# Matmul operands begin 96 bytes, instead of 64, in front of the weights' place modulo 256

## The chip, the core and the metric

The kernel runs on one core of one Trainium2 chip. The metric is the device time of one execution in microseconds. Before the change three runs took 1768.28, 1770.12 and 1774.59 us; the median is 1770.12.

## The reference, cut to what matters

Two models are computed one after the other for 256 tokens of 1024 numbers each, all in float32:

```
h = x
h = h + mamba2_mixer(rmsnorm(h))          # chunked state-space mixer: in, scan, out
h = h + conv_glu_ffn(rmsnorm(h))          # (silu(conv(h @ w_gate)) * (h @ w_up)) @ w_down, width 2816
h = h + fox_attention(rmsnorm(h))         # 16 heads with forget gates
h = h + conv_glu_ffn(rmsnorm(h))
h = rmsnorm(h)
h = [meta; h]                             # 16 meta tokens in front
h = h + [attention(latents); conv_group] @ w_out
h = h + peer_ffn(rmsnorm(h))              # 8 heads x 16 of 16384 experts: gelu(u . x) * gate, times v
out = rmsnorm(h)[16:272]
```

Nearly all of it is products of x with large weights. The experts are computed densely: every u is multiplied with every token (the U pass), the result is multiplied with gates that are zero but for the chosen experts, and then with every v (the V pass).

## The kernel before

**Three matmuls for one.** TensorE's one-pass float type (F32R) keeps fewer bits than float32. So each number is split into a high part of that type and a low part, the rest, and the helper `three` (L361 to L364) issues high by high, high by low and low by high. Profile lines L362, L363 and L364 are these three. A matmul here has a loaded operand of 128 x 128 and a moving operand that streams past it; in the profile's names `ps<-xc,hi` the moving one stands first. Each matmul has a weight load (PEld) of its own, which runs under the matmul before it.

**Weights.** They come from HBM in units of 128 x 2048 numbers (1 MB), in order, into a ring of three buffers `raw`. ScalarE writes the high part into `hi` (L584, L1549), GpSimd (POOL) the low part into `lo` (L759), and TensorE reads both. In the expert passes the units are halves of 1024 columns and two of the ring's buffers are used; ScalarE's part is L1767, the low part is POOL's in the U pass (L798) and VectorE's in the V pass (L2472). SyncE issues the loads when the slot's raw data have been split. The engines' orders are written out by hand and tied together with semaphores; a few loops have many rounds.

**Partners.** `pe_a` (L366) loads weights and streams x (`xc`, `xcl`: 8 chunks of 128 x 256). `pe_b` (L380) loads x and streams 256 weight columns. `pe_w` (L394) loads weights and streams the output halves `oh`, `ol` of a mixer, or the feed-forward products `hdh`, `hdl`. For the second model x has 272 columns (`xh`, `xl`, L165 and L167), rows of 1088 bytes; its query units stream weights of 256 or 160 columns, its convolution units stream 272 columns of x. `u_half` (L1329) is the U pass: 8 triples for each half unit; in its middle part each half unit is followed by gate products four small float32 matmuls (L1326). `v_pair` (L1377) is the V pass: it loads `wgh`, `wgl` (the gated activations, 128 of 256 tokens at a time) and streams 512 columns of `hi`, `lo`.

**Places.** All buffers of SBUF are placed by hand. `sb` puts a buffer at the running place and advances it by the buffer's bytes per partition, rounded up to 32; `to(n)` (L148) advances it to the next byte that is n modulo 256. `raw`, `hi` and `lo` begin at 128 modulo 256, `h` and `acc` too. `xh` and `xl` begin at 64 modulo 256 (`xc` and `xcl` lie in the same memory), and so do `xn`, `oh`, `ol`, four `tmp`, `ones` and the buffers of each phase, `hdh` and `hdl` among them (`xdh`, `xdl` for the routing weights as well). All steps from one chunk to the next are multiples of 256 bytes, but for the 1088 of `xh` and `xl`. The second pair of `wgh`, `wgl` lies in x's memory, 64 bytes on, at 128 modulo 256, as the first pair.

Of the kernel before, what the change touches and what calls it, by code (L numbers as in the profile page):

```python
# [16 lines left out]
F32R = mybir.dt.float32r  # L17
# [7 lines left out]
P = 128  # L25
D = 1024
KC = D // P
SEQ = 256
# [102 lines left out]
def build(nc, A, out):  # L131
# [3 lines left out]
    def sb(name, shape, dt=F32, at=None):  # L135
        size = int(np.prod(shape[1:])) * (2 if dt == BF16 else 4)
        size = (size + 31) // 32 * 32
        off = place["at"] if at is None else at
        t = nc.alloc_sbuf_tensor_at(name, shape, dt, offset=off)
        if at is None:  # L140
            place["at"] += size
        return t
# [5 lines left out]
    def to(offset):  # L148
        place["at"] += (offset - place["at"]) % 256
# [10 lines left out]
    for s in range(2):  # L160
        lo.append(sb(f"lo{s}", [P, UNIT], F32R))
    rs = sb("rs", [P, 3, 32])
    to(64)
    xh_at = place["at"]
    xh = sb("xh", [P, KC, T2], F32R)  # L165
    xl_at = place["at"]
# [8 lines left out]
    lo.append(sb("lo2", [P, UNIT], F32R))  # L175
    h = sb("h", [P, KC, SEQ])
    acc = sb("acc", [P, 2, SEQ])
    to(64)
    xn_at = place["at"]
    xn = sb("xn", [P, NT, D])  # L180
    oh = sb("oh", [P, 2, 2, SEQ], F32R)
# [7 lines left out]
    rrow = sb("rrow", [P, T2])  # L189
    rc = sb("rc", [P, 8])  # L190
    rows = sb("rows", [P, NROWS])
    to(64)
    phase = place["at"]

    def start_phase():
# [104 lines left out]
    hot_at = place["at"]  # L300
# [4 lines left out]
    assert place["at"] <= nc.sbuf_usable_end, (place["at"], nc.sbuf_usable_end)  # L305

    act_in = [sb(f"act_in{i}", [P, 2, SEQ], at=hot_at + 2048 * i) for i in range(2)]
    wgh = [sb(f"wgh{i}", [P, 2, SEQ], F32R, at=(hot_at + 4096, xh_at + 64)[i]) for i in range(2)]
    wgl = [sb(f"wgl{i}", [P, 2, SEQ], F32R, at=(hot_at + 6144, xh_at + 64 + 2048)[i]) for i in range(2)]

    hf = sb("hf", [P, NT, D], at=gates_at)
    gfin = sb("gfin", [P, D], at=gates_at + 8192)
# [2285 lines left out]
```

## Time and profile before

| | |
|---|---|
| three runs | 1768.28, 1770.12, 1774.59 us |
| median | 1770.12 us |
| profiled execution: its span | 1774.7 us |
| granted TensorE clock, mean | 0.978 |
| PE, PEld busy | 1710.5 us (96%), 1606.4 us (91%) |
| DVE, ACT, POOL busy | 1044.9, 826.9, 900.8 us |
| DMA | 310.79 MB, 175 GB/s in the mean |

The profiled execution's own time is its span, 1774.7 us, from the first to the last instruction; it stands beside 1774.59, the slowest of the three runs. PE is busy nearly throughout, but matmuls overlap, so that busy time says little of its pace: a matmul of 256 columns is shown as some 280 ns long and the next begins after less than half of that. The distance between starts is what to read, in a timeline or from the count in a stretch.

The stretches are, in us from the start: the state-space mixer to 245, the first feed-forward part to 441, fox attention to 611, the second feed-forward part to 802, the second model's mixer to 958, routing among other work and the U pass from 995 to 1413, the V pass to the end.

### The profile page before, as it was taken

How to read it: one execution, taken by the hardware profiler on the slowest of the kernel's cores; microseconds unless marked ns; L12 is line 12 of the kernel's file. 1: busy time of each engine (PE TensorE's matmuls, PEld its weight loads, DVE VectorE, ACT ScalarE, POOL GpSimd, SP SyncE). 2: the span in 40 equal slices, each digit the busy share in tenths (PEclk: the TensorE clock that was granted, in tenths of full speed). 3: DMA queues.
4: the chain of work that ended last, by engine and by line, in shares of the span. 5: the costliest groups of instructions: out<-in, count | busy, mean ns of one | idle time of the engine just before them, and what ended most of it. 6: DMA issues, size and time to landing. Idle time of an engine off the chain costs nothing. (4 is left out here: it accounts for less than half of the span.)

```text
span 1774.7 us, 34933 instructions
## 1 busy us (share of the span) xinstructions
PE 1710.5 (96%) x12583; PEld 1606.4 (91%) x12583; DVE 1044.9 (59%) x2198; ACT 826.9 (47%) x1147; POOL 900.8 (51%) x275
## 2 busy tenths in 40 slices
PE   8899799999999999999998999999999999999997
PEld 8889799999997999999678999999999978888886
DVE  7857654345344554344885891745555377777776
ACT  4578343334547433345435544644444443333332
POOL 4676468887682378876205588776666500000000
PEclk9999999999998999999988999999999999999999
DMA  5443335555452245554202466665555687777774
GB/s 212 143 144 118 113 126 190 190 188 192 143 190 72 72 167 190 188 183 160 93 1 84 164 234 236 210 205 177 178 177 177 216 266 240 240 241 243 239 242 160
DMA packets 77453, 310.79 MB, mean 175 GB/s; under 512 B 8768, under 2 KB 10304, under 8 KB 60736
## 3 DMA queue, kind: packets, MB, share of 16 engines
q1 hardware_dynamic: 75024, 306.14, 51.3%
q10 hardware_dynamic: 2352, 3.59, 0.6%
q8 instruction: 52, 0.85, 0.2%
q14 instruction: 25, 0.20, 0.0%
HBM read 290.82 MB, written 18.87 MB: 175 GB/s over the span
## 5 line engine op out<-in xcount | busy, mean ns | idle before, releaser
L759 POOL TENSOR_TENSOR lo<-raw,hi 128x2048 fp32r<-128x2048 f32 x127 | 584.3, 4610 | 378.1 <-ACT hi L584 306.0
L362 PE MATMUL ps<-xc,hi 128*128 128x256 f32 x1912 | 544.3, 285 | 5.7 <-DVE ps L2052 3.3
L363 PE MATMUL ps<-xcl,hi 128*128 128x256 f32 x1912 | 536.3, 280 | 0.0
L364 PE MATMUL ps<-xc,lo 128*128 128x256 f32 x1912 | 536.1, 280 | 0.0
L362 PEld LDWEIGHTS ps<-xc,hi 128*128 128x128 f32 x1912 | 362.6, 190 | 8.6 <-issue 6.9
L798 POOL TENSOR_TENSOR lo<-raw,hi 128x1024 fp32r<-128x1024 f32 x128 | 304.7, 2404 | 128.8 <-ACT hi L1767 128.7
L363 PEld LDWEIGHTS ps<-xcl,hi 128*128 128x128 f32 x1912 | 364.3, 191 | 0.1
L1767 ACT ACTIVATE hi<-raw 128x1024 fp32r<-128x1024 f32 x256 | 264.9, 1058 | 211.3 <-PE ps L364 199.0
L364 PEld LDWEIGHTS ps<-xc,lo 128*128 128x128 f32 x1912 | 360.6, 189 | 0.0
L2472 DVE TENSOR_TENSOR lo<-raw,hi 128x1024 fp32r<-128x1024 f32 x128 | 156.4, 1222 | 81.1 <-ACT hi L1767 81.0
L362 PE MATMUL ps<-hi,wgh 128*128 128x512 f32 x512 | 199.4, 389 | 1.8 <-DVE wgl L2483 1.8
L363 PE MATMUL ps<-lo,wgh 128*128 128x512 f32 x512 | 199.2, 389 | 0.0
L364 PE MATMUL ps<-hi,wgl 128*128 128x512 f32 x512 | 199.2, 389 | 0.0
L584 ACT ACTIVATE hi<-raw 128x2048 fp32r<-128x2048 f32 x65 | 124.5, 1915 | 68.1 <-PE ps L364 66.8
L1805 ACT ACTIVATE act_out<-ps 128x512 f32<-128x512 f32 x64 | 38.3, 598 | 200.9 <-PE ps L364 200.7
L1549 ACT ACTIVATE hi<-raw 128x2048 fp32r<-128x2048 f32 x60 | 114.4, 1907 | 13.2 <-PE ps L364 13.2
L2044 DVE TENSOR_TENSOR ps<-ps,rrow 128x512 f32<-128x512 f32 x44 | 30.8, 699 | 145.8 <-PE ps L364 145.7
L362 PEld LDWEIGHTS ps<-hi,wgh 128*128 128x128 f32 x512 | 96.1, 188 | 22.5 <-issue 1.6
L2453 DVE TENSOR_TENSOR oj<-iota,ps 128x512 f32<-128x512 f32 x64 | 44.0, 688 | 121.9 <-PE ps L1326 120.9
L1544 ACT ACTIVATE fcv<-fcv 128x256 f32<-128x256 f32 x44 | 18.4, 419 | 207.1 <-DVE fcv L2050 207.1
L364 PEld LDWEIGHTS ps<-hi,wgl 128*128 128x128 f32 x512 | 96.1, 188 | 20.0
L363 PEld LDWEIGHTS ps<-lo,wgh 128*128 128x128 f32 x512 | 96.1, 188 | 19.7
(497 smaller groups left out, 3426.6 us busy)
## 6 DMA issues: line engine op xcount, KB each, us to landing
raw<-in_w_u SPq DMA_DIRECT2D x128, 512.0 KB, 4.3
raw<-in_w_v SPq DMA_DIRECT2D x128, 512.0 KB, 4.2
raw<-in_w_up SPq DMA_DIRECT2D x44, 1024.0 KB, 4.8
raw<-in_w_down SPq DMA_DIRECT2D x22, 1024.0 KB, 4.7
raw<-in_w_fox SPq DMA_DIRECT2D x16, 1024.0 KB, 5.0
act_save<-act_out SPq DMA_DIRECT2D x64, 256.0 KB, 2.1
act_in<-act_save SPq DMA_DIRECT2D x64, 256.0 KB, 3.2
raw<-in_w_xbc SPq DMA_DIRECT2D x12, 1024.0 KB, 5.0
```

Of the source, the lines that this page charges most:

```text
L362: pe.matmul(o, ah, bh, start=start, stop=False)
L363: pe.matmul(o, ah, bl, start=False, stop=False)
L364: return pe.matmul(o, al, bh, start=False, stop=stop)
L584: nc.scalar.activation(hi[slot][:], raw[slot][:], ACT.Copy).then_inc(hi_done, 1)
L759: return g.tensor_tensor(lo[slot][:], raw[slot][:], hi[slot][:].bitcast(F32), ALU.subtract)
L798: g.tensor_tensor(lo[q // 2][:, part], raw[q // 2][:, part], hi[q // 2][:, part].bitcast(F32), ALU.subtract).then_inc(u_lo_done, 1)
L1549: s.activation(hi[slot][:], raw[slot][:], ACT.Copy).then_inc(hi_done, 1)
L1767: nc.scalar.activation(hi[s][:, q], raw[s][:, q], ACT.Copy).then_inc(e_hi_done, 1)
L1805: nc.scalar.activation(act_out[s][:].rearrange("p a b -> p (a b)"), ps[:, s, :], ACT.Gelu).then_inc(a_gelu, 1)
L2044: v.tensor_tensor(both, both, bc(rrow[:, META:], 1, [P, 2, SEQ]), ALU.mult).then_inc(f_chain, 1)
L2453: return v.tensor_tensor(place[b][:], iota[:].unsqueeze(1).broadcast_to([P, GT, P]), number, ALU.is_equal)
L2472: v.tensor_tensor(lo[s][:, q], raw[s][:, q], hi[s][:, q].bitcast(F32), ALU.subtract).then_inc(v_lo_done, 1)
```

## The change

The three `to(64)` become `to(32)`, and the second pair of `wgh`, `wgl` is put 96 instead of 64 bytes behind the beginning of x's memory. Nothing else is touched; no instruction is added or taken away.

```diff
@@ -160,7 +160,7 @@
     rs = sb("rs", [P, 3, 32])
-    to(64)
+    to(32)
     xh_at = place["at"]
@@ -175,7 +175,7 @@
     acc = sb("acc", [P, 2, SEQ])
-    to(64)
+    to(32)
     xn_at = place["at"]
@@ -189,7 +189,7 @@
     rows = sb("rows", [P, NROWS])
-    to(64)
+    to(32)
     phase = place["at"]
@@ -305,8 +305,8 @@
-    wgh = [sb(f"wgh{i}", [P, 2, SEQ], F32R, at=(hot_at + 4096, xh_at + 64)[i]) for i in range(2)]
-    wgl = [sb(f"wgl{i}", [P, 2, SEQ], F32R, at=(hot_at + 6144, xh_at + 64 + 2048)[i]) for i in range(2)]
+    wgh = [sb(f"wgh{i}", [P, 2, SEQ], F32R, at=(hot_at + 4096, xh_at + 96)[i]) for i in range(2)]
+    wgl = [sb(f"wgl{i}", [P, 2, SEQ], F32R, at=(hot_at + 6144, xh_at + 96 + 2048)[i]) for i in range(2)]
```

## Rows read from the trace of the kernel before

**Rows 1.** The page: span; chain that ended last, by line.

```profile
span 1774.7 us, 34933 instructions
...
PE ps L362 13%; PE ps L363 13%; PE ps L364 13%; PE ps L1326 3%; DVE eq L2441 1%; DVE eq L2443 1%; DVE sel L2444 1%; DMA act_in<-act_save 0%; POOL lo L798 0%; POOL lo L759 0%; ACT hi L584 0%; DVE h L2319 0%; ACT hi L1767 0%; DVE hf L2505 0%; DVE xdl L478 0%
```

**Rows 2.** Stretches: length, busy us (instructions) of PE, PEld, DVE, ACT, POOL; PEclk, DMA.

```profile
271.40:435.30 163.90, 163.90 (x1394) 163.90 (x1393) 69.51 (x140) 64.07 (x54) 134.23 (x30) 1.00 0.53 187
638.30:802.30 164.00, 164.00 (x1395) 164.00 (x1395) 69.60 (x140) 64.17 (x55) 134.37 (x30) 1.00 0.53 186
468.20:485.60 17.40, 17.40 (x151) 17.40 (x149) 8.52 (x37) 10.15 (x13) 14.30 (x4) 1.00 0.48 166
485.70:523.90 38.20, 38.20 (x338) 38.20 (x338) 20.72 (x86) 18.84 (x21) 31.59 (x8) 1.00 0.54 188
1001.30:1114.30 113.00, 113.00 (x959) 113.00 (x960) 69.28 (x307) 51.57 (x62) 96.42 (x41) 1.00 0.68 229
1159.40:1387.30 227.90, 227.90 (x1986) 227.90 (x1986) 116.75 (x186) 107.86 (x156) 149.29 (x64) 1.00 0.53 179
1391.00:1412.90 21.90, 21.90 (x196) 21.90 (x195) 3.44 (x5) 10.60 (x14) 14.29 (x6) 1.00 0.76 257
```

**Rows 3.** Groups by line and shape: names, shapes, count, busy us, mean ns, idle.

```profile
L362 PE MATMUL ps<-xc,hi 128*128 128x256 f32 x1912 | 544.3, 285 | 5.7 <-DVE ps L2052 3.3 <-issue 0.8 <-POOL lo L798 0.5
...
L362 PE MATMUL ps<-hi,wgh 128*128 128x512 f32 x512 | 199.4, 389 | 1.8 <-DVE wgl L2483 1.8
...
L362 PE MATMUL ps<-hi,xc 128*128 128x256 f32 x384 | 109.4, 285 | 0.3 <-DVE xcl L478 0.2
...
L362 PE MATMUL ps<-hdh,hi 128*128 128x256 f32 x352 | 98.9, 281 | 0.0
```

**Rows 4.** Timeline of PE between gate products: start us, us, instruction.

```profile
1159.79 0.28 PE L362 MATMUL ps<-xc,hi 128*128 128x256 f32 x1
...
1161.91 0.28 PE L362 MATMUL ps<-xc,hi 128*128 128x256 f32 x1
...
1163.52 0.28 PE L362 MATMUL ps<-xc,hi 128*128 128x256 f32 x1
...
1165.56 0.28 PE L362 MATMUL ps<-xc,hi 128*128 128x256 f32 x1
```

**Rows 5.** Timeline of PE at half clock.

```profile
812.39 0.41 PE L362 MATMUL ps<-hi,xh 128*128 128x256 f32 x1
...
813.03 0.41 PE L362 MATMUL ps<-hi,xh 128*128 128x256 f32 x1
```

**Rows 6.** Timeline of PE in the V pass.

```profile
1449.93 0.39 PE L362 MATMUL ps<-hi,wgh 128*128 128x512 f32 x1
...
1451.97 0.39 PE L362 MATMUL ps<-hi,wgh 128*128 128x512 f32 x1
```

**Rows 7.** The page, DMA issues: count, KB each, us to landing.

```profile
act_save<-act_out SPq DMA_DIRECT2D x64, 256.0 KB, 2.1
```

**Rows 8.** Timeline of PE, 272 columns, first of triples k=4 onward.

```profile
825.86 0.29 PE L362 MATMUL ps<-xh,hi 128*128 128x272 f32 x1
...
826.23 0.29 PE L362 MATMUL ps<-xh,hi 128*128 128x272 f32 x1
...
826.62 0.29 PE L362 MATMUL ps<-xh,hi 128*128 128x272 f32 x1
...
826.99 0.29 PE L362 MATMUL ps<-xh,hi 128*128 128x272 f32 x1
...
827.37 0.29 PE L362 MATMUL ps<-xh,hi 128*128 128x272 f32 x1
```

**Rows 9.** Timeline of PE, 160 columns.

```profile
818.92 0.28 PE L362 MATMUL ps<-hi,xh 128*128 128x160 f32 x1
...
819.92 0.27 PE L362 MATMUL ps<-hi,xh 128*128 128x160 f32 x1
```

**Rows 10.** Timeline of PE, eight convolution taps, full fp32.

```profile
870.11 1.89 PE L1186 MATMUL ps<-hc,diag 128*128 128x256 f32 x8
```

## Prediction

> **What bounds the kernel now.** I read the page's head and its chain of waits first [rows 1]. The span is 1774.7 us and the chain that ended last runs mostly through L362, L363 and L364, 13% each: these are the three matmuls of the helper that multiplies a number split into a high and a low part. So the pace of those matmuls is what counts. The table by stretches [rows 2] shows where: in both feed-forward parts, in the two fox query stretches, in the U pass of the experts and in its end, PE is busy for all of the stretch, and POOL, ACT and DVE for 85% of it at the most. The grouped instructions [rows 3] give the kinds: x (xc, xcl) streams as moving operand past loaded weights 1912 times for each of the three lines, the weights stream past loaded x 384 times, the feed-forward products hdh and hdl 352 times, all with 256 columns, and the V pass streams 512 columns 512 times. (The output halves oh and ol go the way of hdh.)
>
> The mean ns of those groups is no pace, because matmuls overlap. The pace is the distance between starts. In the U pass between the gate products, six triples take 2.12 us in one half unit, 117.8 ns each, and 2.04 us in the next, 113.3 ns each [rows 4]. Both read x from the same place, and weights from places that lie a multiple of 4096 bytes apart. The stretch table agrees (the window and 0.28 us of the matmul already under way, by the count): 117.8, 117.8, 117.1 and 118.1 ns in the first, second, third and fifth row, 113.8 and 113.2 ns in the fourth and the last [rows 2]. So there are two paces at the same offset of 64 bytes, a slow one and a fast one, and most of the time is spent in the slow one.
>
> What would be no excess at all? At half clock, 1.2 GHz, three starts take 0.64 us, 213 ns each [rows 5], which is 256 columns at 1.2 GHz and nothing more. At 2.4 GHz, the granted clock in nearly all the rest, 256 columns are 106.7 ns, so 6.7 or 11.1 ns are lost per matmul and only at full speed. That looks like the moving stream and the weight load, both reading SBUF at once, getting into each other's way. The V pass has both of its streams at 128 modulo 256 and takes 2.04 us for nine [rows 6], 226.7 ns against 213.3: 13.3 ns lost.
>
> **The change, part by part.** No instruction is added, removed or reordered, no wait and no DMA either. It only moves places. x, everything from xn to rows, and every phase's buffers begin 32 bytes lower; raw, hi, lo, h and acc stay, because the allocator rounds to 128 again behind x. With the sizes in the listing nothing else shifts: each of the three stops falls 32 bytes earlier and nothing wraps to the next 256.
>
> The weights for the V pass stay too: wgh1 and wgl1 lie at xh's place plus 64, now plus 96, which is 128 in both. V is 1536 matmuls [rows 3] at 226.7 ns, 348 us, and I cost it at nothing. act_out slides 32 bytes, and its 64 stores of 256 KB take 2.1 us each [rows 7], in a pass that needs 5.5 us or more for a unit, so a store that took twice as long would be hidden. DVE and ACT instructions on moved buffers read and write from another place; in the PE-bound stretches DVE is busy at most 61% of the time and ACT 58% [rows 2], so they could grow by half before they set the pace.
>
> What is left is the pace of some 8,000 matmuls of 256 columns. No row has its streams at 96 bytes apart, so I bound it by rows at other distances. The 272-column matmuls of the last block are of use: a row of x is 1088 bytes, so its place advances by 64 bytes with each k. Their triples take 0.37 us at minus 64, 0.39 at 0, 0.37 at plus 64 and 0.38 at 128 (k from 4 to 7) [rows 8]; without loss each would take 0.34. So place does matter, it repeats after 128 bytes as far as this shows, 64 (modulo 128) is the better and 0 the worse, by about 5 ns a matmul. A distance of 96 is 32 modulo 128: just between the two that are known.
>
> The lower end: with 160 columns the stream would take 67 ns, yet nine starts take 1.00 us, 111.1 ns each [rows 9]. There the weight load sets the pace, and no 256-column matmul can go below it by much. All at 111.1 ns: the four slow stretches, 163.9 + 164.0 + 17.4 + 113.0 = 458.3 us, lose 6.7 parts in 117.8, 26 us; the two fast ones, 38.2 + 21.9 us, lose 1.2; the gate stretch has about 31 pairs of half units (227.9 us, 3.73 from 1159.79 to 1163.52 for one with its gate products), of 24 matmuls each, 31 x 24 x (6.7 + 2.2) ns = 6.6 us; the rest some 4. That is 38 us less. The upper end is the worst triple, 0.39 us or 130 ns for 272 columns, 16.7 ns lost, so 123.3 ns for 256: 21 + 5 + 31 x 24 x (5.5 + 10.0) ns = 12 + 3, 41 us more.
>
> I take the value in between that the rows show to be possible in these very loops: every matmul at 113.3 ns. The four slow stretches give 458.3 x 4.5 / 117.8 = 17.5 us. The slow half units of the gate stretch give 31 x 24 x 4.5 ns = 3.3 us. Elsewhere some 2,000 matmuls of the groups are left; if all were slow and all on the path they would give 9 us, but these are the parts in which the matmuls stand in short runs between waits, and some run at 113.3 ns already, so I take 2. Sum: 23 us. POOL, 134.2 us in a stretch that would shrink from 163.9 to 157.7 us, remains below it. Why should 96 be on the good side? Suppose that a load begins some 3 ns behind the matmul it lies under, less than the timeline resolves: the moving stream, 4 bytes a column at 2.4 GHz, has then run on by some 28 bytes (an estimate). With that lag, 64 behind becomes some 36 behind and 0 becomes 28 ahead, nearly equally near to a meeting, which fits that the two differ so little in rows 8. 96 behind would be 64 to 70 behind, the farthest that two streams can be on a ring of 128 bytes. This is an argument, not a row.
>
> The profiled execution's span, 1774.7 us, is the slowest of the three times shown (1774.59); the median is 1770.1. 1774.7 - 23 gives 1751.7 for a like execution; on the median it is 1747.
>
> A rule of the Trainium skill speaks against all of this: SBUF — State Buffer, section Who interferes with whom, gives TensorE two independent read ports, one for the moving operand and one for weight loads, and says PE and ACT "never wait on anyone". By it the places cannot matter and the time stays at 1770 us. The trace disagrees, 0.37 against 0.39 us with nothing changed but k [rows 8].
>
> **The rivals.**
>
> No effect: the pace is set by how each run of matmuls happens to begin, not by the distance. For it speaks that both paces occur at one distance in neighbouring half units [rows 4]; against it rows 8. The time would be 1770, within 5 us.
>
> Slower: 96 is nearer to a meeting of the streams than 64. The mechanism: at 32 modulo 128 each load overlaps half of a piece that the moving stream is reading, and the fast pace is no longer reached. For it: linear interpolation in rows 8 between 64 and 0. Its place is the same loops; its price is the V pass's loss of 13.3 ns, so 120.0 ns for each: 458.3 x 2.2 / 117.8 = 8.6, the fast stretches 60.1 x 6.7 / 113.3 = 3.6, the gate stretch 31 x 24 x (2.2 + 6.7) ns = 6.6, the rest 2: 21 us more, 1791. It decides as soon as the mean pace is above the present mean of about 116.7 ns. A start at 32 modulo 64 could add to it by touching one more piece of memory per stream. Against that: eight tap matmuls, each moving its start by 4 bytes, take 1.89 us, (1.89 - 0.38) / 7 = 216 ns for each, the 213 ns of two passes and almost nothing more [rows 10]. But they stream at half the rate.
>
> Conflict gone: the distance is the ideal one and the weight load alone sets the pace: 38 us less, 1732.
>
> **How the numbers follow.** All at the fast pace, 1747 (its own range 1737 to 1762): 0.39. Conflict gone, 1732: 0.09. No effect, 1770: 0.14. Slower, 1791: 0.38. This measurement tells apart about 0.3%, 5 us. Faster is 0.39 + 0.09 = 0.48, the same 0.14, slower 0.38. The range runs from the time of the conflict gone, less 2, to the slower case plus some 6: 1730 to 1797.
>
> **What would show it right or wrong.** The distance of starts in the two feed-forward parts: 113.3 ns and a stretch of 157.7 us for 163.9 if right, 117.8 if nothing changed, 119 or more if the slower rival holds. In the gate stretch both half units would be at 2.04 us. The 272-column triples should be alike for all k, since each is now 32 from both known distances (modulo 128). The V pass must keep 226.7 ns, and the half-clock matmuls 213 ns. The prediction is wrong if the feed-forward parts are not shorter, and its sum is wrong if they are and the gain is lost in a wait for POOL's low parts.

## The result: 1% slower, and the profile after

After the change the median is 1787.5 us (1784.1 to 1789.8, 5 runs), beside 1770.1 us before (1766.8 to 1780.2, 5 runs beside them). The ratio is 1.0092, interval 1.0064 to 1.0121. The forecast was 1747 us, so it had the wrong sign. What came is the rival "slower" (1791 us), and 1787.5 lies inside the range that was given.

The page of the kernel after: span, busy time of PE and the chain that ended last.

```profile
span 1787.9 us, 34933 instructions
...
PE 1724.0 (96%) x12583; PEld 1622.1 (91%) x12583; DVE 1043.8 (58%) x2198; ACT 826.3 (46%) x1147; POOL 900.2 (50%) x275
...
PE ps L362 13%; PE ps L364 13%; PE ps L363 13%; PE ps L1326 3%; DVE eq L2443 1%; DVE eq L2441 1%; DVE sel L2444 1%; PE ps L1306 0%; DMA raw<-in_w_v 0%; DVE h L2319 0%; ACT hi L1767 0%; DVE xdl L478 0%; DVE hf L2505 0%; DVE acc L492 0%; ACT hi L584 0%
```

The chain is that of [rows 1]: the same three matmuls, the same shares. No new wait stands in it. PE is busy 13.5 us longer than the 1710.5 us of before, and the span is 13.2 us longer, at nearly the same mean granted clock (0.978 before, 0.979 after): the matmuls themselves are further apart.

The stretches after, in the columns of [rows 2]: first feed-forward part, second one, two stretches of fox queries, the plain part of the U pass, its gate part and its end.

```profile
276.30:439.70 163.40, 163.40 (x1395) 163.40 (x1394) 69.60 (x140) 64.18 (x55) 134.37 (x30) 1.00 0.53 188
646.60:811.80 165.20, 165.20 (x1394) 165.20 (x1394) 69.57 (x140) 64.14 (x55) 134.40 (x30) 1.00 0.52 185
474.00:493.00 19.00, 19.00 (x161) 19.00 (x160) 9.44 (x41) 11.31 (x13) 14.52 (x4) 1.00 0.49 167
494.00:533.00 39.00, 39.00 (x327) 39.00 (x326) 18.34 (x75) 18.05 (x21) 31.36 (x7) 1.00 0.53 185
1012.00:1125.00 113.00, 113.00 (x966) 113.00 (x965) 69.48 (x290) 52.01 (x62) 94.95 (x40) 1.00 0.67 229
1167.50:1396.50 229.00, 229.00 (x1958) 229.00 (x1957) 115.19 (x184) 105.32 (x153) 146.32 (x62) 1.00 0.52 176
1400.00:1423.00 23.00, 23.00 (x197) 23.00 (x196) 0.06 (x1) 10.67 (x14) 15.88 (x7) 1.00 0.65 224
```

The pace is the window and 0.28 us by the count, as in the prediction. The two feed-forward parts are at 117.3 and 118.7 ns, both 117.8 before. The fox queries, where x is the loaded operand, are at 119.8 and 120.1 ns, before 117.1 and 113.8 [rows 2]. The plain U part is at 117.3 (118.1), the end of U at 118.2 (113.2). POOL, DVE and ACT do in the feed-forward parts what they did before, to 0.2 us.

The gate stretch after, timeline of PE (start us, us, instruction): second triple of a half unit and the beginning six triples later, then the same of the next half unit.

```profile
1167.67 0.28 PE L362 MATMUL ps<-xc,hi 128*128 128x256 f32 x1
...
1169.80 0.28 PE L362 MATMUL ps<-xc,hi 128*128 128x256 f32 x1
...
1171.41 0.28 PE L362 MATMUL ps<-xc,hi 128*128 128x256 f32 x1
...
1173.55 0.28 PE L362 MATMUL ps<-xc,hi 128*128 128x256 f32 x1
```

Six triples take 2.13 and 2.14 us, 118.6 ns a matmul in the mean, where 2.12 and 2.04 alternated in [rows 4]. The fast half unit is gone.

Half clock and V pass, timeline of PE: three starts at half clock, nine in the V pass.

```profile
820.65 0.41 PE L362 MATMUL ps<-hi,xh 128*128 128x256 f32 x1
...
821.29 0.41 PE L362 MATMUL ps<-hi,xh 128*128 128x256 f32 x1
...
1459.74 0.39 PE L362 MATMUL ps<-hi,wgh 128*128 128x512 f32 x1
...
1461.78 0.39 PE L362 MATMUL ps<-hi,wgh 128*128 128x512 f32 x1
```

0.64 us and 2.04 us, as in [rows 5] and [rows 6]: nothing moved there. The 272-column triples from k=4 on, timeline of PE:

```profile
835.33 0.29 PE L362 MATMUL ps<-xh,hi 128*128 128x272 f32 x1
...
835.70 0.29 PE L362 MATMUL ps<-xh,hi 128*128 128x272 f32 x1
...
836.08 0.29 PE L362 MATMUL ps<-xh,hi 128*128 128x272 f32 x1
...
836.45 0.29 PE L362 MATMUL ps<-xh,hi 128*128 128x272 f32 x1
...
836.83 0.28 PE L362 MATMUL ps<-xh,hi 128*128 128x272 f32 x1
```

0.37, 0.38, 0.37, 0.38 us, against 0.37, 0.39, 0.37, 0.38 [rows 8]. The stores of [rows 7] still land in 2.1 us.

Where the 13.2 us of the two profiled executions arise, by the start of the same matmul in both traces: before the first product with hdh +4.9 (271.4 to 276.3), first feed-forward part -0.6, up to the first product with oh in fox +3.2, from there to the second feed-forward part +0.8, that part +1.2, second model's mixer -1.3, up to the U pass -0.1, U pass +5.1 (995.3 to 1412.9; 1003.5 to 1426.1), V pass and the rest 0. The profiled execution of before was one of its slower ones (1774.7); the medians are 17.4 us apart.

The same by kind of matmul, from all starts of 256-column matmuls that follow each other by less than 140 ns in the two traces: with x streaming the mean distance went from 116.7 to 118.1 ns (some 5,600 matmuls, 8 us), with x loaded from 116.3 to 119.9 ns (some 1,100, 4 us), with the output halves streaming from 116.0 to 118.2 ns (some 700, 1.6 us), with the feed-forward products from 117.8 to 118.0 ns (1056, 0.2 us).

### The profile page after: what moved, and what is told of

It reads as the page before. It is cut to its first block and busy times, and to the rows that moved or that the text cites. A ratio compares the mean times of both kernels' runs of the same rounds, so it can differ in the third digit from the quotient of the medians.

```text
span 1787.9 us, 34933 instructions
## 1 busy us (share of the span) xinstructions
PE 1724.0 (96%) x12583; PEld 1622.1 (91%) x12583; DVE 1043.8 (58%) x2198; ACT 826.3 (46%) x1147; POOL 900.2 (50%) x275
```

## Experiments

**The matmuls alone.** No other engine and no wait: blocks of 48 matmuls of 256 columns in the kernel's order (high by high, high by low, low by high). "Distance" is from here on the start of the moving operand minus that of the loaded one, in bytes, modulo 256. "In front" means at a lower place, "behind" at a higher one. x 64 bytes in front of the weights, as before, is distance 192 where x streams, and the change makes it 160; where x is loaded, the two distances are 64 and 96. The code is shortened; the same run also had blocks with x loaded, blocks of 512 columns, and both operands slid together.

```python
def loads_w(dw, dx):            # in bytes / 4
    for f in range(2):
        for k in range(8):
            three(ps[:, 0, f*256:(f+1)*256], w[256*k + 128*f + dw :][:128], x[256*k + dx :][:256])
for d in range(0, 256, 16): 3 x loads_w(0, d // 4)
```

> Matmuls alone, nothing else running: triples of F32R matmuls with a weight load each, in the kernel's pattern, with the moving operand 0, 16, ... 240 bytes (modulo 256) behind the loaded one; three blocks of 48 per distance with 256 columns and weights loaded, two with x loaded and weights moving, one block of 24 with 512 columns, and then both operands slid together by 0 to 240 bytes at a fixed distance of 64. It computes none of the reference. Theory (the distance modulo 128 or 256 sets how long the stream and the load get in each other's way): the distance between starts varies with the distance in bytes, near 120 ns at 96 in front with x loaded, 117 to 119 with weights loaded, 113.3 or 117.8 at 64; sliding both together changes nothing. Rival (a start at 32 modulo 64 costs, whatever the distance): starts at 32 modulo 64 are slower than their neighbours in both sweeps, also when both operands slide together. Rival (other engines and DMAs set the pace): all distances show the same, at or near 106.7 ns.

Stretches of one block each, with PE and PEld busy (ACT and POOL have none): distances 0, 96, 112, 112, 160, 192 and 192.

```profile
29.31:35.38 6.07, 6.01 (x48) 5.81 (x49) 0.00 (x0) 0.00 (x0) 1.00 0.00 0
137.15:143.22 6.07, 6.01 (x48) 5.80 (x49) 0.00 (x0) 0.00 (x0) 1.00 0.01 3
155.37:161.15 5.78, 5.72 (x49) 5.53 (x49) 0.00 (x0) 0.00 (x0) 1.00 0.02 3
161.15:166.95 5.80, 5.74 (x49) 5.55 (x49) 0.00 (x0) 0.00 (x0) 1.00 0.00 0
208.99:214.96 5.97, 5.91 (x49) 5.71 (x49) 0.00 (x0) 0.00 (x0) 1.00 0.00 0
245.06:250.84 5.78, 5.72 (x48) 5.53 (x48) 0.00 (x0) 0.00 (x0) 1.00 0.00 0
250.84:256.82 5.98, 5.92 (x49) 5.72 (x49) 0.00 (x0) 0.00 (x0) 1.00 0.01 3
```

Nothing runs beside the matmuls, and still these blocks take between 5.78 and 6.07 us. A block has a start-up and a settling of some matmuls; its second half is steady. Timeline of PE at distance 96, then at 112, nine matmuls each:

```profile
139.76 0.28 PE L60 MATMUL ps<-xhi,whi 128*128 128x256 f32 x1
...
140.84 0.29 PE L60 MATMUL ps<-xhi,whi 128*128 128x256 f32 x1
...
155.83 0.28 PE L60 MATMUL ps<-xhi,whi 128*128 128x256 f32 x1
...
156.85 0.28 PE L60 MATMUL ps<-xhi,whi 128*128 128x256 f32 x1
```

1.08 us by 9 is 120.0 ns, 1.02 by 9 is 113.3. The mean distance of starts in the second half of each block, all from the same trace (ns; a second figure where blocks of one distance differ):

```
distance   0: 120.0         16: 118.6, 113.3  32: 116.7         48: 118.3
          64: 117.8         80: 118.3, 120.0  96: 120.0        112: 113.3
         128: 118.6, 120.0 144: 118.6-118.8  160: 117.4, 118.8 176: 119.3
         192: 113.3, 117.8 208: 119.2, 116.7 224: 118.3        240: 117.2
x loaded:  64: 117.8         96: 120.0        112: 116.7       144: 119.9
         192: 113.3, 117.8
512 columns, x loaded: distance 0 226.6, 16 226.7, all others 228.6 to 234.6
```

These are the kernels' own figures: before 113.3 and 117.8 (192), after 117.4 and 118.8 (160) where the weights are loaded, 120.0 (96) where x is. One figure is missing in the sweep: at distance 64 with x loaded it has 117.8 in both blocks, but the kernel before ran its fox queries at 113.8 from 485.7 to 523.9 us [rows 2]. So this distance has the fast pace too, and a few blocks of a sweep need not show both. The loss comes from the places of TensorE's own two operands, not from a conflict with other engines, and it follows a jagged curve. 96 and 224 differ, and so do 112 and 240: the curve does not repeat after 128 bytes. The V pass was at its best place already. With both operands slid together by 0 to 240 bytes in steps of 16 at 192, the blocks were at 113.3 or 117.8 ns. It was not quite the same everywhere: slid by an odd multiple of 16 all 16 blocks had 113.3; slid by an even one the first block of each pair had 113.3 and the second 117.8, eight times out of eight. The Trainium skill (SBUF — State Buffer, section Who interferes with whom) says that PE never waits on anyone. The trace does not bear that out for TensorE alone: by the places of its own two operands the same matmul goes from 113.3 to 120.0 ns.

**Both sides moved by 32.** The distance stays at 192 and only the place modulo 64 changes (edits shortened).

```diff
-    to(128)        # three times
+    to(96)
-    to(64)         # three times
+    to(32)
```

> Weights and partners both 32 bytes lower (weights at 96, partners at 32 modulo 256), so the distance is 64 again and every start lies at 32 modulo 64. Theory (distance): as the kernel before, 1770 us, ratio 1.000 within 0.003, starts 113.3 or 117.8 ns apart in the steady loops. Rival (place modulo 64): as the changed kernel or slower, ratio 1.009 or more, V pass above 226.7 ns.

Measured: 1763.5 us (1758.1 to 1776.2, 12 runs), ratio 0.9975 (0.9947 to 1.0003); before, run beside it, 1769.7 (1758.5 to 1778.5, 23 runs). The new place modulo 64 costs nothing, and the V pass keeps 226.7 ns. The first feed-forward part in this profile:

```profile
274.10:431.00 156.90, 156.90 (x1387) 156.90 (x1386) 68.57 (x138) 63.28 (x53) 133.26 (x30) 1.00 0.55 195
```

157.18 by 1387 is 113.3 ns: the fast one of the two paces of 192, throughout. One profile at 192 can therefore not be compared with another to better than the spread of the runs, 20 us.

**x alone, and all but x.** The first of the three `to(64)` holds x (and wgh, which is put 96 further instead of 64); the other two hold output halves and feed-forward products.

```diff
# x alone
-    to(64)      # in front of xh_at
+    to(32)
```

```diff
# all but x
-    to(64)      # in front of xn_at, and in front of phase
+    to(32)
```

> Only x goes to 96 in front of the weights; output halves, feed-forward products, the routing's x and the small buffers stay at 64. Theory (distance, each group of matmuls by itself): the fox query units at 120.0 ns, gate stretch at 118.8 ns, as in the changed kernel; hdh and oh units as before, 117.8 or 113.3. Most of the 17 us come from it: 8 to 15 us slower than before. Rival (the loss comes from DVE, ACT or POOL instructions on the other buffers that moved): as before, 1770 us.

> The other half of the change alone: output halves, feed-forward products and all phase buffers at 96 in front, x at 64. Theory (distance): hdh and oh units at 117.3 or 118.7 ns, gate stretch alternates 113.3 and 117.8 as before, fox query units 113.3 to 117.8; 0 to 6 us slower than before. Rival (other engines' instructions on moved buffers): nearly all of the 17 us, 1787 us.

Measured: x alone 1783.3 us, ratio 1.0090 (1.0061 to 1.0119); all but x 1770.4 us, ratio 1.0000 (0.9978 to 1.0022). x alone carries the loss, within what these runs resolve: by the medians 13.6 us of the 17.4, by the ratios all of it (1.0090 and 1.0092), and all but x adds nothing, to 4 us either way. Both came within what was expected by the distance, and the rival of other engines' instructions on moved buffers is refuted. x is in 1912 + 384 of the triples with 256 columns, hdh in 352 [rows 3]. The second feed-forward part with all but x moved, a window of 163.6 us:

```profile
635.40:799.00 163.60, 163.60 (x1388) 163.60 (x1386) 68.75 (x138) 63.39 (x53) 133.58 (x30) 1.00 0.52 186
```

118.1 ns, a mixture of x streams at 192 and hdh streams at 160.

**A finer sweep.** Distances off the multiples of 16, distance 112 with different beginnings, and fewer loaded columns (code shortened).

```python
for d in range(8, 256, 16): 2 x loads_w(0, d // 4)
for d in (100, 104, 108, 112, 116, 120, 124): 3 x loads_w(0, d // 4)
for gap in range(8):
    for d in (112, 192, 160): rest(gap); loads_w(0, d // 4)     # rest: gap short matmuls and a wait
for d in (0, 96, 112, 192):
    for c in (128, 96, 64, 32): 2 x part(c, d // 4)             # c loaded columns
```

> Matmuls alone again; computes none of the reference. First the odd multiples of 8 bytes, then 100 to 124 in steps of 4, then eight rounds of 112, 192 and 160, each after another short run of matmuls so that each block begins differently, and last the loaded operand with 128, 96, 64 and 32 columns at the distances 0, 96, 112, 192. Distances are the moving operand's start minus the loaded one's, modulo 256. Theory (the stream is held up by the weight load): with fewer loaded columns the loss shrinks, to 106.7 ns at 32 columns; 112 gives 113.3 ns in every one of the eight rounds, 192 gives 113.3 in some and 117.8 in others, 160 gives 117.3 or 118.8; around 112 a window some 16 bytes wide is at 113.3. Rival (a fixed cost for each matmul, only its size depends on the place): the loss is the same for 32 loaded columns as for 128.

Steady paces: odd multiples of 8 bytes 117.5 to 122.2 ns, most at 120; 108 120.0, 112 113.3, 116 121.8, 120 122.2, 124 117.8 to 119.8. With eight beginnings 112 gave 113.3 each time, 192 gave 113.3 six times and 117.8 twice, 160 gave 117.3 six times and 118.8 twice. With 128, 96, 64 and 32 loaded columns: 120.0, 116, 113.3, 117.8 at distance 0; 113.3, 117.8, 116.7, 113.3 at 112. The timeline of PE at 112, nine matmuls, and at 116, six:

```profile
279.96 0.28 PE L60 MATMUL ps<-xhi,whi 128*128 128x256 f32 x1
...
280.98 0.28 PE L60 MATMUL ps<-xhi,whi 128*128 128x256 f32 x1
...
298.57 0.28 PE L60 MATMUL ps<-xhi,whi 128*128 128x256 f32 x1
...
299.30 0.28 PE L60 MATMUL ps<-xhi,whi 128*128 128x256 f32 x1
```

113.3 and 121.7 ns, 4 bytes apart. So the fast pace at 112 is a single place, not a window of 16 bytes as expected, and it does not depend on the beginning. The steadiness at 112 was foreseen; the part on the weight load did not hold: a load of 32 columns reads a quarter as much, and the loss neither vanishes nor shrinks in order. That the two streams meet is not shown by it, only that their places matter.

**The kernel with x 112 bytes behind the weights (distance 112).** Buffers begin at 224 modulo 256 and 16 bytes of each are skipped, so that the operands begin at 240. hdh, oh, xdh and their low parts alike; the second wgh and wgl stay at 128 (edits shortened).

```diff
-    to(64)
+    to(224)
-    xh = sb("xh", [P, KC, T2], F32R)
+    xh = sbx("xh", [P, KC, T2], at=xh_at)     # [P, n + 8], elements 4 to 4 + n
```

> x, output halves, feed-forward products and the routing's x begin 112 bytes behind the weights' place (240 modulo 256), by starting 16 bytes into buffers at 224; V pass unchanged. Theory (the curve that matmuls alone showed): 113.3 ns in all loops that load weights: feed-forward stretches 157.7 us instead of 163.9, gate stretch with all half units at 2.04 us; the units that load x (fox queries) have the distance 144 and take 118.5 to 120 ns. Against the kernel before 17 to 20 us less from the first and 4 more from the second: 1753 to 1757 us, ratio 0.990 to 0.993. Rival (the curve of matmuls alone does not carry over once other engines run): within 0.3% of before.

Measured: 1756.9 us (1756.3 to 1761.1, 6 runs), ratio 0.9926 (0.9897 to 0.9955): faster than both kernels, at the upper end of what was expected, and the 6 runs are 5 us apart instead of 14 (13 runs of before, 1762.9 to 1777.2). Its first feed-forward part, its fox queries, and in the timeline of PE the matmuls 4, 13 and 22 of a half unit between gate products:

```profile
273.10:431.00 157.90, 157.90 (x1396) 157.90 (x1395) 69.53 (x140) 64.29 (x55) 135.45 (x30) 1.00 0.56 194
```

```profile
494.00:533.00 39.00, 39.00 (x327) 38.84 (x326) 13.51 (x56) 20.39 (x25) 30.74 (x8) 1.00 0.52 176
```

```profile
1162.65 0.28 PE L372 MATMUL ps<-xc,hi 128*128 128x256 f32 x1
...
1163.71 0.28 PE L372 MATMUL ps<-xc,hi 128*128 128x256 f32 x1
...
1164.73 0.28 PE L372 MATMUL ps<-xc,hi 128*128 128x256 f32 x1
```

Feed-forward 113.3 ns. The gate half unit begins at 117.8 (1.06 us for nine) and reaches 113.3 (1.02) only after a dozen matmuls. So six triples take 2.08 us in every half unit, not the 2.04 that was expected, and that is the mean of the 2.12 and 2.04 that alternated before [rows 4]: the gate stretch gains nothing. The fox queries, with x loaded at distance 144, are at 120.1: the sweep has 119.9 there.

Not all of the 13.8 us need be pace. The mean granted clock was 0.981 over these six runs and 0.979 over the 13 of before. A mean clock that is 0.0024 higher is some 8 us less at half clock in a run, and that is worth 4 us at the most (an estimate from these figures). The record does not say why the clock differs.

**The same with fox's x at 64 modulo 256**, to take that loss back (edits shortened).

```diff
+    xcf = sb("xcf", [P, KC, SEQ], F32R, at=xh_at + 96)
-    pe_b(pe, (U_FQ + n) % RING, ...)
+    pe_b(pe, (U_FQ + n) % RING, ..., x=(xcf, xcfl), ...)
```

> As the last, but fox attention's x lies at 64 modulo 256, as in the kernel before, so that its query units have their old distance. Theory: fox query units back at 113.3 to 117.8 ns, 3 to 5 us less than without: 1749 to 1753 us. Rival: no difference from the last.

Measured: 1759.8 us (1758.5 to 1762.2), ratio 0.9938 (0.9915 to 0.9961), so by the medians 3 us behind the last one instead of 3 to 5 ahead; the runs of the two overlap. The same window:

```profile
494.00:533.00 39.00, 39.00 (x332) 38.77 (x331) 13.82 (x58) 19.33 (x23) 31.77 (x8) 1.00 0.55 189
```

118.3 ns instead of 120.1: the queries end 1.8 us earlier (533.6 for 535.4), at 117.8, not at the 113.3 that half of them had before. After that PE waits 3.93 us in both kernels, and from the end of this wait to the first product with oh the attention is 3.7 us longer here (45.9 us for 42.2). The granted clock accounts for it. Two stretches in a row of each trace, with PEclk as the third figure from the end, first of the last kernel, then of this one:

```profile
540.20:547.00 6.80, 5.85 (x25) 5.06 (x26) 1.74 (x4) 5.16 (x20) 3.16 (x1) 0.50 0.38 123
547.00:553.80 6.80, 6.80 (x54) 5.87 (x53) 4.14 (x14) 5.14 (x20) 0.00 (x0) 1.00 0.09 36
```

```profile
540.20:547.00 6.80, 6.80 (x28) 5.72 (x29) 1.83 (x5) 3.56 (x14) 1.39 (x1) 0.50 0.45 154
547.00:553.70 6.70, 6.70 (x32) 6.11 (x30) 2.51 (x8) 3.88 (x14) 0.00 (x0) 0.50 0.01 4
```

Around that wait the clock fell to half (PEclk 0.50), and it came back after 6.8 us in the one and after 13.6 us in the other, where PE got through 32 matmuls instead of 54. Over all runs the mean granted clock is 0.978 here and 0.981 in the kernel with distance 112 throughout. So the queries did gain their 1.8 us, and the clock took back more. Whether fox's place has to do with the clock is not shown.

**Partners at distance 0.** Everything at 128 modulo 256.

```diff
-    to(64)
+    to(128)      # three times, wgh at xh_at + 0
```

> Weights and partners both at 128 modulo 256, distance 0. Theory (distance): 120.0 ns everywhere with 256 columns: slower than the kernel before by 20 to 30 us, 1790 to 1800 us, ratio 1.011 to 1.017. Rival (nearer to 0 is only slightly worse than 96, as interpolation between 64 and 0 had it): 1787.

Measured: 1799.3 us (1797.7 to 1801.3), ratio 1.0160 (1.0132 to 1.0189). First feed-forward part:

```profile
276.70:440.00 163.30, 163.30 (x1363) 163.30 (x1363) 66.56 (x134) 61.35 (x48) 130.94 (x29) 1.00 0.52 185
```

120.0 ns. In the long loops the curve measured with the matmuls alone predicts the kernel at three places: 112, 160 and 0. It does not say which of two paces a loop takes, and not what short runs of matmuls do, such as the gate half units.

**Is it the distance or the place?** Both operands slid together in small steps (code shortened).

```python
for d in (112, 192, 160, 0):
    for slide in (0, 4, 8, 12, 16, 32): 3 x loads_w(slide // 4, (d + slide) // 4)
for d in (116, 120, 124):
    for slide in (4, 8, 12): 2 x loads_w((16 - slide) // 4, (d + 16 - slide) // 4)
```

> This kernel computes none of the reference: it only runs blocks of 48 matmuls with the split weights loaded and the split x streaming (256 columns), as the first sweep does. Question: at 116 bytes the pace was 121.8 ns and at 112 it was 113.3, but both the distance and the start of x had left a multiple of 16 bytes. Now both operands are slid together by 0, 4, 8, 12, 16 and 32 bytes at the distances 112, 192, 160 and 0, three blocks each; then distances 116, 120 and 124 with x on a multiple of 16 bytes and the weights off it, and with both off it. Theory (only the distance counts): every slide at 112 stays at 113.3 ns, at 192 at 113.3 or 117.8, at 160 at 117.3 or 118.8, at 0 at 120.0; and 116 to 124 stay at 118 to 122 wherever x starts. Rival (each operand touches a piece of 16 bytes more when it starts between two of them): slides by 4, 8 and 12 cost 119 to 122 ns at 112 and at 192, slides by 16 and 32 cost nothing, and distances 116 to 124 with x on a multiple of 16 are better than the ones with both off it.

One block each, distance 112 with a slide of 0, 8, 16 and 32 bytes:

```profile
34.01:39.83 5.82, 5.76 (x49) 5.56 (x49) 0.00 (x0) 0.00 (x0) 1.00 0.00 0
70.44:76.67 6.23, 6.17 (x48) 5.96 (x48) 0.00 (x0) 0.00 (x0) 1.00 0.01 3
106.59:112.68 6.09, 6.03 (x49) 5.82 (x49) 0.00 (x0) 0.00 (x0) 1.00 0.01 3
124.57:130.39 5.82, 5.76 (x49) 5.56 (x49) 0.00 (x0) 0.00 (x0) 1.00 0.00 0
```

Steady paces at 112: 113.3, 122.2, 123.9, 116.5 for slides of 0, 4, 8, 12; 116.7 and 120.0 at 16; 113.3 at 32. At 192: 113.3, 121.1, 120.9, 117.5, then 113.3 at 16 and 32. At 160 slides of 4 to 12 gave 120.0 to 123.3, the others 117.3 to 118.5; at 0 a slide of 4 gave 122.3, one of 16 118.3, and the rest 120.0 as without. Both theories missed. The place does count, but only below 32 bytes: a slide of 32 changes nothing. A start between multiples of 16 costs in most cases, not in all (at distance 0 slides of 8 and 12 are free), and at 112 it also matters which of the two is on a multiple of 32 (the loaded one must be; it agrees with the first sweep's 116.7 at 112 with x loaded, where x was the one off 32). Neither rule is complete: at distance 116, with x on a multiple of 32 and the weights 4 bytes short of a multiple of 16, it was 116.7 instead of the finer sweep's 121.8. The Trainium skill (SBUF — State Buffer, section Door 1: The DMA port swizzle) has SBUF in lines of 16 bytes, each crossing to a new line paying; the cost of most starts off 16 (121.7 for 113.3 ns above) goes that way, but the free slides at distance 0 do not, and it leaves the curve at multiples of 16 unexplained.

## Why the prediction was wrong

**What failed** is the step "every matmul at 113.3 ns". It was 117.3 to 118.8 with the weights loaded and 120.0 with x loaded. In the terms of the sum: the four slow stretches were to give 17.5 us, and the two feed-forward parts among them came out at -0.6 and +1.2 us; the gate stretch was to give 3.3 us, and its 64 half units took 3.75 us each for a mean of 3.68 before, some 4 us more. The step stood on two things. The first was the reading that the loss "repeats after 128 bytes". Rows 8 show four points of a circle of 256, 64 bytes apart, with a resolution of 10 ns for three matmuls; they cannot show a period, and nothing between the points. The sweep has 113.3 at 112 and 117.2 at 240. The second was the lag of 3 ns by which 96 would be "the farthest that two streams can be". No row bore it, and the sweep refutes it: 96 in front of the loaded weights (160) is at 117.4 or 118.8, no better than 64 in front, and 96 behind a loaded x is among the worst, 120.0. An argument that was said to be "not a row" was given the largest single chance. Why the pace follows this curve stays open: the runs show that the places of the two operands set it, and no model here explains it.

**The rival "slower"** had the sign, and 1791 us is near 1787.5. Its size came out partly by luck. It priced every matmul at 120.0 ns: true of the fox queries (120.0) only. The feed-forward parts were to lose 2.2 ns each and came out at -0.4 and +0.9; the part ahead of them, for which 2 us with all of the rest were allowed, lost 4.9. Both its mechanism, half of a piece shared at 32 modulo 128, and its extra (a start at 32 modulo 64) are refuted: 32 itself is at 116.7, better than 64, and both sides at 32 modulo 64 cost nothing (0.9975). What was held against the extra was misread, too: the 31 taps leave 62 records in the trace, two each, so the eight of rows 10 are four matmuls, and the start moves by 4 bytes only at every second record.

**"No effect"** was wrong as to the time, but its mechanism is half true: at 192 and at 160 a block settles into one of two paces (six of eight against two). At 112, with the loaded operand on a multiple of 32, every block had the one pace, and so at 0 with both operands unslid. That the beginning selects the pace is likely, since nothing else differed, but each beginning was run once. So the kernel before was a mixture of the two paces of 192, and the change replaced it by the two of 160, both slow.

**Right steps.** PE's pace is what bounds the kernel: PE busy +13.5 us, span +13.2. The V pass keeps 226.7 ns. Half clock keeps 213 ns. Nothing else that moved cost anything that these runs resolve: all but x gives 1.0000, to 0.2% either way. The 272-column triples are alike to 10 ns, but not for the reason given; their distances after are 160, 224, 32 and 96, and the sweep has 117.4, 118.3, 116.7 and 120.0 for these. The feed-forward test was set up badly: "117.8 if nothing changed, 119 or more if slower" left the measured 117.3 below all but the fast case and 118.7 between the other two. That the good pace is reachable in these loops was right too: at 112 the feed-forward parts are at 113.3, and 13.8 us of the 23 forecast are there (1770.7 to 1756.9), up to 4 of them perhaps from the clock. But 96 was not the place for it.

## What to carry to other kernels

With a weight load under each 256-column matmul, measure the pace against the distance of the two operands' starts modulo 256, in steps of 16 bytes, with the matmuls alone, several blocks for each distance: it costs one run and predicts the long loops of the kernel. Two or four points of such a curve are no basis for a fifth. Prefer a place with one pace (112 here) over one that is fast in some rounds: the median fell by 14 us, and the runs were 5 us apart (6 runs) instead of 14 (13 runs). Such a place may exist at 192 as well, with both operands on an odd multiple of 16: all 19 blocks of it were at 113.3, but no kernel was run with it. Before a difference of a few microseconds is put down to a place, compare the mean granted clock of the runs.

## What the runs showed of the hardware

- The pace of the same matmul lies between 113.3 and 123.9 ns by the places of its operands alone, nothing else running and at full granted clock.
- At distance 192 two steady paces exist, 113.3 and 117.8 ns, and each persists for whole feed-forward parts (156.9 us at 113.3 in one kernel, 163.9 us at 117.8 in another [rows 2]).
- Four bytes can cost 8.4 ns (112 against 116), and a common slide of 16 bytes 3.3 to 6.7 ns at 112 and nothing at 192.
- With 512 columns the best distances are 0 and 16 (226.6 and 226.7 ns, the others 228.6 to 234.6, one block each), with 256 columns 0 is among the worst (120.0).
- After the same wait of 3.93 us of PE the granted clock stayed at half for 6.8 us in one kernel and 13.6 us in another, and the attention took 42.2 and 45.9 us.
